# A transformer block on one Trainium2 core: modulation and first projection in four quarters of the contraction

## The reference

```python
mod = silu(c) @ w_ada + b_ada                    # 1024 x 6144
sh1, sc1, g1, sh2, sc2, g2 = split(mod, 6)
h = rmsnorm(x, norm_gains[0]) * (1.0 + sc1) + sh1
proj = h @ w_in                                  # 1024 x 2304: qa, ka, va, qb, kb, vb
out = concat(moba_attention(qa, ka, va), swa_attention(qb, kb, vb, sinks)) @ w_out
x = x + g1 * rmsnorm(out, norm_gains[1])
```

## Time and profile before

| | us |
|---|---|
| median of three executions | 789.35 |
| profiled execution, its own time | 793.4 |
| its span, first to last instruction | 791.7 |
| TensorE (PE) busy | 739.5 (93%) |
| VectorE (DVE) busy | 518.5 (65%) |
| ScalarE (ACT) busy | 449.5 (57%) |
| GpSimd (POOL) busy | 44.3 (6%) |
| mean granted TensorE clock | 0.976 |

### The profile page before, as it was taken

The page is one execution under the profiler, slowest core; times in us unless marked ns, Lnnn a source line. Parts: engine busy times, 40 slices in busy tenths (PEclk is TensorE's granted clock), DMA queues, the critical chain, the costliest instruction groups (busy, mean ns, idle before and its releaser), DMA issues.

```text
span 791.7 us, 12079 instructions
## 1 busy us (share of the span) xinstructions
PE 739.5 (93%) x4062; PEld 622.0 (79%) x4062; DVE 518.5 (65%) x764; ACT 449.5 (57%) x724; POOL 44.3 (6%) x77
## 2 busy tenths in 40 slices
PE   0599999979999999997999999999897999999998
PEld 0498966679999887775989777777686888888886
DVE  6886697678777744348657465665656777677443
ACT  1644677566666443355555587654546777777331
POOL 3100100100000100014102000000000000000000
PEclk9899999969999999999999999999997999999999
DMA  8999985237877655443774554544444566666651
GB/s 319 362 352 319 261 275 161 80 112 218 246 221 250 225 190 184 159 126 102 225 190 130 185 168 135 167 119 135 157 131 132 168 190 176 203 174 201 201 198 55
DMA packets 137166, 150.50 MB, mean 190 GB/s; under 512 B 6163, under 2 KB 111782, under 8 KB 137128
## 3 DMA queue, kind: packets, MB, share of 16 engines
q1 hardware_dynamic: 135278, 145.28, 59.2%
q10 hardware_dynamic: 1852, 4.75, 1.7%
HBM read 148.57 MB, written 1.44 MB: 189 GB/s over the span
## 4 chain that ended last, share of the span: by engine, by line
PE 85%; DVE 6%; ACT 3%; DMA 3%; issue 2%; POOL 0%; SPq 0%; POOLq 0%; DVEq 0%; ACTq 0%
PE acc L1363 14%; PE acc L1365 13%; PE acc L1364 13%; PE acc L1355 11%; PE acc L1342 7%; PE acc L1343 7%; PE acc L1344 7%; PE acc L1356 5%; DMA raw<-in_w_ada 3%; PE aux L1331 2%; PE aux L1527 1%; DVE wl L960 1%; PE aux L1501 1%; PE aux L1496 1%; DVE ada_sum L1038 1%
## 5 line engine op out<-in xcount | busy, mean ns | idle before, releaser
L960 DVE TENSOR_TENSOR wl<-raw,wh 128x1024 fp32r<-128x1024 f32 x217 | 266.0, 1231 | 151.6 <-ACT wh L594 150.8
L594 ACT ACTIVATE wh<-raw 128x1024 fp32r<-128x1024 f32 x217 | 227.9, 1055 | 124.2 <-PE acc L1365 111.3
L1342 PE MATMUL acc<-xT,wh 128*128 128x256 f32 x440 | 127.0, 289 | 5.5 <-DVE xT L990 4.1
L1355 PE MATMUL acc<-xT,wh 128*128 128x512 f32 x352 | 127.1, 405 | 0.8 <-DVE xT L982 0.8
L1343 PE MATMUL acc<-xT,wh 128*128 128x256 f32 x440 | 126.2, 287 | 0.0
L1344 PE MATMUL acc<-xT,wl 128*128 128x256 f32 x440 | 126.2, 287 | 0.0
L1363 PE MATMUL acc<-wh,xT 128*128 128x512 f32 (+1 forms) x272 | 110.0, 404 | 4.7 <-DVE xT L982 2.4
L1365 PE MATMUL acc<-wh,xT 128*128 128x512 f32 (+1 forms) x272 | 105.5, 388 | 0.0
L1364 PE MATMUL acc<-wl,xT 128*128 128x512 f32 (+1 forms) x272 | 105.2, 387 | 0.0
L1356 PE MATMUL acc<-xT,wl 128*128 128x256 f32 x352 | 100.1, 284 | 0.0
L1342 PEld LDWEIGHTS acc<-xT,wh 128*128 128x128 f32 x440 | 86.3, 196 | 7.5 <-issue 5.9
(11 more groups left out here) (260 smaller groups left out, 889.8 us busy)
## 6 DMA issues: line engine op xcount, KB each, us to landing
raw<-in_w_in SPq DMA_DIRECT2D x66, 512.0 KB, 3.6
raw<-in_w SPq DMA_DIRECT2D x64, 512.0 KB, 3.8
raw<-in_w_ffn_in SPq DMA_DIRECT2D x44, 512.0 KB, 4.4
raw<-in_w_ada SPq DMA_DIRECT2D x27, 512.0 KB, 6.2
raw<-in_w_ffn_out SPq DMA_DIRECT2D x22, 512.0 KB, 3.3
raw_more<-in_w_ada SPq DMA_DIRECT2D x13, 512.0 KB, 6.7
raw<-in_w_out SPq DMA_DIRECT2D x13, 512.0 KB, 4.3
rows_tmp<-in_w_ada ACTq DMA_DIRECT2D x8, 512.0 KB
```

The lines of the kernel that those rows point to most:

```text
L594: A(wh[:, s, :], raw_unit, ACT.Copy).then_inc(rounded, 1)
L960: V.tensor_tensor(wl[:, s, :], raw_slot(r), wh[:, s, :].bitcast(f32), ALU.subtract).then_inc(split_ready, 1)
L1342: mm(bank[:, 0:ROWS], wh[:, s, w], hi, start=(kt == 0), stop=False)
L1355: mm(bank[:, :], wh[:, s, w], moving[:, kt, :], start=(kt == 0), stop=False, skip_group_check=True)
```

## The change

The 16 first w_ada units and weight units 0 to 11 are regrouped by quarters of the contraction, 256 of 1,024 each.

- A w_ada unit of the first 16 is now two rows-of-128 blocks by 256 columns of sh1 and the same 256 of sc1. Four units complete shift and scale for a quarter. Each is two transfers of 256 KB with 1 KB pieces and, on VectorE, two multiply-adds of 512 columns with a wait behind each (`ada_first`). They land in eight slots inside `dbias`, `qT`, `kT` and `vall`, which attention uses only later; the ring of six holds the weight units and the other 24 w_ada units. The first part of `dbias` is loaded behind weight unit 9, once w_ada unit 11 has been used.
- A weight unit u = 3q + j is now quarter q of the contraction for 512 columns of q (j=0), k (j=1) or values (j=2). `block_unit` adds it to two `acc` banks with 24 matmuls of 256 columns, `value_half` to `aux[2]` and `aux[3]`. All sums stay in PSUM over the four quarters.
- TensorE's order is: transposes of x and of the sums for quarter 0, block 0, transposes of x for quarter 1, the product for the distance bias, block 1, transposes of the sums for quarter 1, values 2, block 3, and so on. Shift and scale of a quarter are summed by one reduction on VectorE.
- GpSimd makes the remainders of units 0, 2, 5 and 8. Their raw slots count as free when VectorE has made the next unit's remainder.
- x goes behind the second w_ada unit, b_ada's first part from ScalarE, and the copies to attention's tensors are taken at units 9, 10 and 11. Fewer of the later w_ada units stand before unit 15 and more behind it.
- The small loads and memsets of ScalarE and GpSimd move behind the first norm.

```diff
 def ada_after(u):
-    return {5: 1, 6: 1, 7: 1, 8: 1, 9: 1, 10: 1, 11: 1, 12: 1, 13: 1, 14: 1, 15: 1, 16: 1, 17: 2, 18: 2, 19: 2, 20: 3, 21: 3}.get(u, 0)
+    return {9: 1, 10: 1, 11: 1, 12: 1, 13: 1, 14: 1, 15: 2, 16: 2, 17: 2, 18: 3, 19: 3, 20: 3, 21: 3}.get(u, 0)
...
+QUARTERS = KT // 2
+EARLY_SLOTS = 8
+POOL_LOW = [0, 2, 5, 8]
 def first_stream():
-    order = [("ada", i) for i in range(ADA_FIRST)]
+    order = [("ada", i) for i in range(4)]
     i = ADA_FIRST
     for u in range(U_UP1):
+        q, j = divmod(u, 3)
+        if q >= 1 and q < QUARTERS and j == 0:
+            order.append(("ada", 4 * q + 3))
         order.append(("w", u))
+        if u == 3 * q and q < QUARTERS - 1:
+            order.append(("ada", 4 * q + 4))
+        if u == 3 * q + 1 and q < QUARTERS - 1:
+            order += [("ada", 4 * q + 5), ("ada", 4 * q + 6)]
         order += [("ada", i + j) for j in range(ada_after(u))]
...
-BIAS_AFTER = [5, 17]
+BIAS_AFTER = [9, 17]
+X_AFTER = 1
-PLACE = {item: place for place, item in enumerate(STREAM)}
+RING_ITEMS = [item for item in STREAM if item[0] == "w" or item[1] >= ADA_FIRST]
+PLACE = {item: place for place, item in enumerate(RING_ITEMS)}
...
+        def early_slot(i):
+            s = i % EARLY_SLOTS
+            if s < 4:
+                return dbias[:, 4 * s:4 * s + 4, :].rearrange("p h n -> p (h n)")
+            if s < 6:
+                return qT[:, 4 * (s - 4):4 * (s - 4) + 4, :].rearrange("p t n -> p (t n)")
...
+        def quarter_columns(src, q):
+            return src.rearrange("p (c n) -> p c n", c=2)[:, :, ROWS * q:ROWS * (q + 1)]
...
+                if kind == "ada" and k < ADA_FIRST:
+                    q, j = divmod(k, 4)
+                    if k >= EARLY_SLOTS:
+                        sp.wait_ge(ada_used, k - EARLY_SLOTS + 1)
+                    for t in range(2):
+                        sp.dma_start(early_slot(k)[:, 512 * t:512 * (t + 1)].rearrange("p (c n) -> p c n", c=2),
+                                     quarter_columns(w_ada[:, 2 * j + t, 0:2 * D], q)).then_inc(early_full[k % EARLY_SLOTS], 16)
...
+                elif k < 3 * QUARTERS:
+                    q, j = divmod(k, 3)
+                    sp.dma_start(slot.rearrange("p (t n) -> p t n", t=2),
+                                 w_in[:, 2 * q:2 * q + 2, W_A * j:W_A * (j + 1)]).then_inc(done, 16)
...
-                if place == 0:
-                    sp.wait_ge(ada_zeroed, 2)
-                    sp.dma_start(ada_sum[0:1, 0:2 * D], a["b_ada"][:, 0:2 * D]).then_inc(ada_bias, 16)
-                if place == 2 * RING - 1:
+                if (kind, k) == ("ada", X_AFTER):
                     for r in range(RT):
-                        sp.dma_start(x[:, r, :], x_dram[:, r, :]).then_inc(x_loaded, 16)
+                        sp.dma_start(x[:, r, :], x_dram[:, r, :]).then_inc(x_loaded[r], 16)
                 if kind == "w" and k in BIAS_AFTER:
                     sp.wait_ge(dist_stored, 16)
                     half = BIAS_AFTER.index(k)
+                    sp.wait_ge(ada_used, EARLY_SLOTS + 4)
...
+            def low_unit(u):
+                pool.wait_ge(rounded, u + 1)
+                s = slot_of(u)
+                nc.gpsimd.tensor_tensor(wl[:, s, :], raw_slot(raw_place(u)[0]), wh[:, s, :].bitcast(f32), ALU.subtract)\
+                    .then_inc(low_by_pool, 1)
+            for u in POOL_LOW:
+                low_unit(u)
+            nc.gpsimd.memset(G2[:, :], 0.0).then_inc(g2_used, 1)
...
+            def from_transposed_pair(q, scale, bias):
+                act.wait_ge(mod_ready, q + 1)
+                act.wait_ge(nt_ready, q + 1)
+                if q >= 2:
+                    act.wait_ge(xT_ready, 4 * (q - 1))
+                for t in range(2):
+                    kt = 2 * q + t
+                    A(tmpT[:, kt % 4, :], aux[0][:, ROWS * t:ROWS * (t + 1)], ACT.Identity,
...
-            for k in range(11):
-                round_static(k + AHEAD)
-                leave_bank(k)
+            for u in (10, 11, 12):
+                round_static(u)
+            leave_bank(9)
+            round_static(13)
+            leave_bank(10)
+            round_static(14)
             leave_bank(11)
-            round_static(11 + AHEAD)
...
+            def ada_first(i):
+                q, j = divmod(i, 4)
+                dve.wait_ge(early_full[i % EARLY_SLOTS], 32 * (i // EARLY_SLOTS + 1))
+                if i >= 1:
+                    dve.wait_ge(ada_used, i)
+                sums = quarter_columns(ada_sum[:, 0:2 * D], q)
+                for t in range(2):
+                    product = early_slot(i)[:, 512 * t:512 * (t + 1)].rearrange("p (c n) -> p c n", c=2)
+                    ins = V.scalar_tensor_tensor(out=sums, in0=product, scalar=cT[:, 2 * j + t:2 * j + t + 1], in1=sums,
+                                                 op0=ALU.mult, op1=ALU.add)
+                    if t == 0:
+                        link(ins)
+                ins.then_inc(ada_used, 1)
...
+            def input_scale(q):
+                dve.wait_ge(mod_psum, q + 1)
+                cols = slice(2 * q, 2 * q + 2)
+                V.reduce_sum(modT[:, 0:2 * KT].rearrange("p (c t) -> p c t", c=2)[:, :, cols],
+                             aux[1][:, :].rearrange("p (c t n) -> p c t n", c=2, t=2), axis=AX.X).then_inc(mod_summed, 1)
...
+            input_scale(0)
+            ada_first(4)
+            split_pair(0)
+            low_static(1)
+            for i in (5, 6, 7):
+                ada_first(i)
+            input_scale(1)
+            low_static(3)
+            split_pair(1)
+            ada_first(8)
+            low_static(4)
+            for i in (9, 10, 11):
+                ada_first(i)
...
+            def block_unit(u):
+                q, j = divmod(u, 3)
+                s = slot_of(u)
+                low_ready(u)
+                pe.wait_ge(xT_ready, 4 * q + 4)
+                for t in range(2):
+                    hi, lo = xT[:, 2 * q + t, 0:ROWS], xT[:, 2 * q + t, ROWS:]
+                    for b in range(4):
+                        bank = acc[2 * j + b // 2][:, ROWS * (b % 2):ROWS * (b % 2 + 1)]
...
+            block_unit(0)
+            to_columns_pair(xr, 1, normed)
+            pe.wait_ge(misc_loaded, 16 * 3)
+            mm(aux[3][0:N_HEADS, 0:DIST], relw[:, :], onehot[:, :], start=True, stop=True).then_inc(dist_done, 1)
+            block_unit(1)
+            transpose_quarter(1)
+            value_half(2, 0)
+            pe.wait_ge(dist_copied, 1)
+            value_half(2, 1).then_inc(unit_done, 1)
+            block_unit(3)
+            to_columns_pair(xr, 2, normed)
...
+            block_unit(6)
+            to_columns_pair(xr, 3, normed)
+            block_unit(7)
+            transpose_quarter(3)
+            value_half(8, 0)
+            value_half(8, 1).then_inc(unit_done, 1)
+            block_unit(9)
+            block_unit(10)
+            value_half(11, 0)
+            value_half(11, 1).then_inc(unit_done, 1)
```

More of the change, by code:

```diff
@@ L661, in _ @@
                 act.dma_start(dst, src).then_inc(vec_loaded, 16)
+            act.wait_ge(ada_zeroed, 2)
+            act.dma_start(ada_sum[0:1, 0:2 * D], a["b_ada"][:, 0:2 * D]).then_inc(ada_bias, 16)
             act.wait_ge(vec_ready, 1)
             A(cT[:, :], vT[:, V_C:V_C + KT], ACT.Silu).then_inc(c_ready, 1)
-            act.wait_ge(ada_zeroed2, 3)
-            act.dma_start(ada_sum[0:1, 2 * D:], a["b_ada"][:, 2 * D:5 * D]).then_inc(ada_bias2, 16)
+            for r in range(RT):
+                act.wait_ge(x_loaded[r], 16)
+                square_rows(N_IN1, r)
+            for r in range(RT):
+                act.wait_ge(rstd_ready, r + 1)
+                A(xr[:, r, :], x[:, r, :], ACT.Copy, scale=rstd[:, N_IN1, r:r + 1]).then_inc(normed, 1)
             act.wait_ge(relw_made, 2)
@@ L1059, in _ @@
             dve.wait_ge(ada_bias2, 16)
-            for k in range(12):
-                low_static(k + AHEAD)
-                for i in ada_units_after(k + AHEAD):
+            for i in ada_units_after(9):
+                ada(i)
+            for u in range(10, 12 + AHEAD):
+                low_static(u)
+                for i in ada_units_after(u):
                     ada(i)
@@ new lines, in _, with low_ready @@
+            to_columns_pair(xr, 0, normed)
+            transpose_quarter(0)
+            def low_ready(u):
+                if u in POOL_LOW:
+                    pe.wait_ge(low_by_pool, POOL_LOW.index(u) + 1)
+                else:
+                    pe.wait_ge(split_ready, u + 1)
+            def block_unit(u):
[3 more added lines that the diff above has]
+                pe.wait_ge(xT_ready, 4 * q + 4)
+                for t in range(2):
+                    hi, lo = xT[:, 2 * q + t, 0:ROWS], xT[:, 2 * q + t, ROWS:]
+                    for b in range(4):
+                        bank = acc[2 * j + b // 2][:, ROWS * (b % 2):ROWS * (b % 2 + 1)]
+                        w = slice(512 * t + P * b, 512 * t + P * (b + 1))
```

(16 more changed lines are left out.)

197 lines of the change are left out of this document (97 added, 100 removed).

## The result

The changed kernel took 800.0 us (median of four executions, 798.85 to 801.03), the kernel before 790.84 beside it on the same chip (four, 789.23 to 792.87): a ratio of 1.0117, with 95% between 1.0098 and 1.0136. It is **9.2 us slower**, above the range of the forecast (782.0 to 797.5). The profiled execution took 798.85, with a span of 797.1.

The account below looks back on a forecast made before the run. It took w_ada's arrival to bound the front and TensorE what follows, with VectorE bounding the new quarters. Attention's +4.8 less the projection's 1.4 gave +3.4 on 789.35, about 792.8 us, range 782 to 797.5.

Parts of the forecast that it names:

- Attention costs 4.8 more: From the projection's end to the last head: late weight units and VectorE's longer list lengthen attention by 4.8 us.
- Units 17 and 18 are late the same way: Early attention: TensorE's projection units cover these late weights; steps of heads 1 and 3 wait some 1.5 us.
- foreseen 80.4: Start of attention: unit 16, issued once its slot frees at 73.3 and behind ten queued transfers, lands near 80.4 us.
- Head 0's 2.3: Head 0's transposes end 13.8 us behind the projection instead of 11.5, because unit 16's rounding precedes the exponential: 2.3 lost.
- up to 1 us: Attention from head 4 on: VectorE needs about 7.25 us per pair against TensorE's 7.12, up to 1 us more overall.
- the dbias transfers cost nothing: Front: dbias transfers wait for w_ada unit 11 and hold SP to 48; unit 10 lands near 53, due at 64.
- Rival 3: TensorE's gap ahead of quarter 3's transposes lowers the granted clock to 1.2 GHz: 796.7 us in total, chance 0.20.
- the 1.72 forecast: w_ada unit on VectorE: two halves of 0.75 us, each with a 0.11 wait, cost 1.72 us.
- The projection's gain: End of the first projection: 71.4 us instead of 72.8, 1.4 gained.
- Rival 1: GpSimd's remainders fall beside VectorE's waits and hold nothing up: projection ends at 64.4, total 785.8 us, chance 0.16.
- Rival 2: TensorE bounds the quarters and attention keeps the lead: projection ends at 62 to 64, total 780 us, chance 0.14.
- Rival 5: w_ada's halves are served slowly, each quarter waits: projection ends after 83 us, total above 800, chance 0.03.

Follow-up runs that it names:

- e6: Changed kernel, with VectorE making unit 15's remainder and its two w_ada adds before waiting for head 0's exponential: 794.52 us, 1.0041 of the kernel before.
- e5: Changed kernel with w_ada units spread: one behind each of units 9 to 17, two behind 18 to 20, three behind 21 to 23: 788.79 us, ratio 0.9970.
- e2: Changed kernel with the bias table's second half sent behind unit 11 instead of unit 17: 798.75 us, 1.0111 of the kernel before.
- e8: Changed kernel with the edits of e6 and e1, and the bias table's second half behind unit 18 instead of 17: 786.85 us, ratio 0.9948.
- e11: Changed kernel with 36 useless matmuls on TensorE between unit 17 and head 2's transposes: 799.66 us, 1.0118 of the kernel before.
- e3: Changed kernel with fewer w_ada units between units 9 to 17 and four or five behind each of 18 to 21: 807.88 us, ratio 1.0217.
- e1: Changed kernel with VectorE making all remainders of the first projection, none on GpSimd: 796.97 us, 1.0072 of the kernel before.

## Why the prediction was wrong

**The step that failed is "Attention costs 4.8 more".** It measured 12.4. Within it, the sentence "Units 17 and 18 are late the same way, but TensorE has projection units as cover there; steps of heads 1 and 3 wait some 1.5" is what fell. I placed unit 16 right in kind (landing 77.5, foreseen 80.4; ScalarE waited 2.96 us for it) and found that its rounding stands ahead of the exponential. I did not follow this on to VectorE: what stands behind head 0's reciprocal there, and whose slot it frees. I had followed the ring for unit 16 alone. Three more steps of the same bookkeeping, from the forecast's own landing at 80.4 (rounding 1.1, table load 1.3, exponentials 1.0, remainder 1.2), give unit 17's issue near 85, against 76.23 before; it measured 82.22. e6 shows 6.4 us for this position, e5 11.6 for the whole of the table. Where the 12.4 us go can be read from the starts of the transposes on TensorE (the projection is 4.1 early, so head 0's 1.9 early is a loss of 2.2):

| transposes of head | before | changed | lost in this step |
|---|---|---|---|
| 0 | 83.81 | 81.96 | 2.2 |
| 1 | 90.93 | 90.43 | 1.4 |
| 2 | 98.41 | 102.37 | 4.5 |
| 3 | 101.04 | 106.56 | 1.6 |
| 4 | 104.82 | 113.14 | 2.8 |
| 15 | 143.21 | 151.58 | 0.1, heads 5 to 15 together |

Head 0's 2.3 was forecast rightly. Heads 1 to 4 lost 10.2 where the forecast had 1.5 for two of them, and the "up to 1 us" from VectorE's longer list in the later heads didn't come (0.1).

**The bias table's second half had no term.** The forecast's sentence that the dbias transfers cost nothing speaks of the first half, and for it no run shows a cost: the DMA engines were down to 159 to 174 GB/s from 44 to 50 us, but the chain of waits holds no transfer between 11 and 60 us. The second half, behind unit 17 in both kernels, was left out. From the earlier trace rows I had 235 GB/s over 4 us; that window ends with the issues, while the transfers went on, as later windows of the kernel before show:

```profile
82.00:84.00 2.00, 2.00 (x19) 2.00 (x18) 2.00 (x6) 1.76 (x5) 0.00 (x0) 1.00 1.16 167
84.00:86.00 2.00, 2.00 (x14) 1.50 (x13) 2.00 (x3) 1.33 (x5) 0.00 (x0) 1.00 1.10 167
```

In e2 the DMA engines ran at 174 GB/s for the 8 us in which half a table was under way. In the changed kernel the second half is issued 6.1 us later than before (82.72, before 76.65), and unit 18 follows its last issue after 1.0 us instead of 4.4 (87.75, before 84.99): 9.27 us to landing, before 6.5. e8 against e6 puts the price of this place at some 3 us.

**The clock was looked for in the wrong gap.** Rival 3 expected 1.2 GHz ahead of quarter 3; in the changed kernel's trace the gaps in the quarters left it at 1.00. It fell in the gap at 98 to 102 us instead, which the forecast didn't have, for 3.4 us by e11's one trace. Rival 3's mechanism is not refuted: in e3 and e6 the clock did fall to 0.50, in the gap ahead of quarter 2's transposes.

**The front, step by step.** A half cost 0.76 us. The wait was not 0.11 behind each half: it was 0.03 inside a unit and 0.09 between two: four halves in 3.18 us, so a unit costs 1.64 with its waits instead of the 1.72 forecast (1.39 before).

The changed kernel's timeline of VectorE, then its chain of waits at two of GpSimd's remainders and at the transposes of two quarters:

```profile
5.43 3.18 DVE L1096 SCALAR_TENSOR_TENSOR ada_sum<-dbias,cT,ada_sum 128x512 f32<-128x512 f32 x4 [0.28 <-ACT cT L711]
```

```profile
37.95 0.76 DVE ada_sum L1096
...
38.81 2.69 DVE ada_sum L1096
...
42.42 0.64 PE aux L1431 x4
...
47.03 2.96 DVE ada_sum L1096
...
55.93 0.67 PE aux L1431 x4
```

- Block 0 started at 19.9, forecast 21.3; the transposes of quarter 2 ended at 43.1 instead of 45.1, those of quarter 3 at 56.6 instead of 59.1. A quarter took 13.5 us (42.42 to 55.93), forecast 14.0. The projection's gain was 4.1 instead of 1.4: the mechanism as described, mis-sized by the smaller wait and the earlier start; of the rest, up to 1.7 us is the movement of the front between kernels.
- GpSimd excluded VectorE: a half took 2.69 and 2.96 us instead of 0.76 beside it, 1.9 and 2.2 more (forecast 2.1 for each). In quarter 1 it held VectorE for 1.9 us too, and there a wait of 2.2 us for TensorE hid it, as forecast (nothing). In quarter 0 it cost 0.9 instead of 1.9, since it began at 14.84, early enough to end at 17.18. The Trainium skill (SBUF — State Buffer, Who interferes with whom) calls the port pair that VectorE and GpSimd share an exclusive lock, and has a VectorE instruction with two inputs in SBUF contend with a GpSimd instruction that reads SBUF; the trace agrees, with these 0.9 to 2.2 us.
- Rival 1 (GpSimd holds nothing up) is refuted by e1. Rival 2 (TensorE bounds the quarters) was not the case: TensorE waited 2.4 and 1.6 us for VectorE ahead of the transposes of quarters 2 and 3. Rival 5 (w_ada's halves served slowly) fell: 353 GB/s up to 36 us, and VectorE's longest wait for w_ada was 2.4 us, for unit 2 at 11 us. The Trainium skill (DMA: Bandwidth & Descriptors, Anatomy of one DMA) gives the 2.0 us as the fixed cost of one DMA, fitted on transfers that GpSimd issues. Adding it up one by one, as rival 5 did, doesn't hold here, with many transfers under way.

Had attention given back 4.8 against the projection's 4.1, the end would have been 0.7 late: 791.5 beside 790.8, within half a percent. That the forecast leaned towards "same" hung on this one step.

## What to carry to other kernels

When a table changes how many items stand between two weights in a ring of slots, write down for each weight of the next stage whose slot it takes, and where the instruction that frees that slot stands on its engine. A release that stands behind a wait for another engine turns one late transfer into a chain of late ones, which no stage's busy share shows. And a helper engine is worth having only where it doesn't exclude the one it helps: four times 2.3 to 2.8 us of GpSimd, to save VectorE 1.2 each, cost 2.9 us in all.

## What the runs showed of the hardware

- VectorE waits for GpSimd even with a tiny instruction. The scaling step of 128x2 elements, 0.16 us in e1, took 1.05 beside GpSimd's remainder (timeline of the changed kernel):

```profile
14.84 2.34 POOL L582 TENSOR_TENSOR wl<-raw,wh 128x1024 fp32r<-128x1024 f32 x1
...
16.14 1.05 DVE L1129 SCALAR_TENSOR_TENSOR A<-modT,vT 128x2 f32<-128x2 f32 x1
```

  Not every instruction waits: the reduction of the sums, whose one input lies in PSUM, took 0.69 us beside the same GpSimd instruction (at 15.41), as it does alone.

- A gap does not always bring the clock down. The changed kernel's TensorE did nothing from 40 to 42 us and kept 1.00; the gap at 98 to 102 us was followed by 0.50 up to 112, with matmuls running. In e3 TensorE was idle ahead of the same transposes, from 41.2 to 43.6 us, and then had 0.50 (windows of the changed kernel, then of e3):

```profile
40.00:42.00 2.00, 0.00 (x0) 0.00 (x0) 1.97 (x2) 0.00 (x0) 0.94 (x1) 1.00 1.09 400
```

```profile
44.00:46.00 2.00, 2.00 (x8) 1.71 (x7) 1.26 (x3) 0.32 (x1) 0.00 (x0) 0.50 0.76 165
```

  Ahead of these transposes the gap is 2.44 us long in both kernels, so its length does not decide between them. e6 has the same gap and 0.50 behind it; the other four kernels with the same front kept 1.00. What decides stays open.
- The granted clock of a row is not always the pace of the matmuls. Block 0 began at 19.92, and until 24.5 us its matmuls followed each other every 0.21 us, from 24.7 on every 0.12, while the rows read 1.00 throughout. The slow start that the forecast counted in for block 0 was there, but not in the clock's row; why is not shown.
- The bias table, read in pieces of 1 KB from overlapping rows of a small region, kept the DMA engines full (share 1.12) at 174 GB/s in e2, where the halves of w_ada, in pieces of 1 KB too, and the weights between them ran at 353. The size of the pieces alone doesn't set the rate. Which of the other differences does (the overlapping source, 16 partitions a transfer) was not tried.
